# Sums of expert outputs by one product per 64 tokens, with loads that join both addends, and constant products around them

## What is computed

```python
y = jnp.zeros((t, dm), x2.dtype).at[flat_tok[order]].add(y_sorted)
...
xp = layer_norm(DEEPNORM_ALPHA * xp + hier_moe(xp, *moe_w), ln2_g[l], ln2_b[l])
```

## Time and profile before

| what | value |
|---|---|
| median of 3 runs | 2174.96 us (2174.8 to 2177.64) |
| the profiled execution | 2183.16 us, span 2181.3 us |
| PE busy | 2072.5 us, 95% of the span |
| DVE, ACT, POOL busy | 805.1, 325.7, 222.1 us |
| mean granted TensorE clock | 0.974 |
| all DMA | 535.92 MB, mean 246 GB/s |

### The profile page before, as it was taken

How to read it: one execution, slowest core, us unless ns; L and a number is a source line. 1 busy time by engine, 2 the same in 40 slices (tenths; PEclk the granted TensorE clock), 3 DMA queues, 4 the chain that set the end, 5 groups by cost and what they waited for, 6 DMA issues and landing times.

```text
span 2181.3 us, 32300 instructions
## 1 busy us (share of the span) xinstructions
PE 2072.5 (95%) x13024; PEld 1221.7 (56%) x13024; DVE 805.1 (37%) x1547; ACT 325.7 (15%) x856; POOL 222.1 (10%) x250
## 2 busy tenths in 40 slices
PE   8999999989999999899799999999999999999986
PEld 5666655565555655455366666555645556554542
DVE  4512166672222222222482123766622221222224
ACT  2011123311111011111010111333001110110103
POOL 1200000000111111110231000000001100111101
PEclk9999999999999999999899999999999999999997
DMA  6601131348999999998634101413689999999956
GB/s 223 193 30 38 41 128 68 113 158 316 360 392 400 414 384 396 392 387 334 231 123 120 39 29 32 158 59 116 228 325 391 399 406 395 392 388 394 379 219 236
DMA packets 77465, 535.92 MB, mean 246 GB/s; under 512 B 14586, under 2 KB 23674, under 8 KB 52386
## 3 DMA queue, kind: packets, MB, share of 16 engines
q1 hardware_dynamic: 64050, 498.37, 59.5%
q0 software_dynamic: 13264, 35.44, 4.8%
HBM read 494.14 MB, written 54.08 MB: 251 GB/s over the span
## 4 chain that ended last, share of the span: by engine, by line
PE 91%; DVE 4%; issue 3%; DMA 1%; ACT 1%; POOL 1%; DVEq 0%; SPq 0%; POOLq 0%
PE ps L925 20%; PE ps L616 19%; PE ps L969 10%; PE ps L763 9%; PE ps L905 6%; PE ps L595 4%; PE ps L893 3%; PE ps L976 3%; PE ps L921 3%; PE ps L949 2%; PE ps L567 1%; PE ps L963 1%; PE ps L569 1%; PE ps L805 1%; PE ps L705 1%
## 5 line engine op out<-in xcount | busy, mean ns | idle before, releaser
L927 PE MATMUL ps<-arena 128*64 128x256 f32 x1920 | 450.9, 391 | 0.0
L925 PE MATMUL ps<-arena 128*64 128x256 f32 x1920 | 450.9, 391 | 0.0
L616 PE MATMUL ps<-arena 128*128 128x344 f32 x1440 | 421.2, 453 | 0.0
L925 PEld LDWEIGHTS ps<-arena 128*64 128x64 f32 x1920 | 255.0, 135 | 175.9 <-issue 23.9
L616 PEld LDWEIGHTS ps<-arena 128*128 128x128 f32 x1440 | 272.0, 190 | 142.9 <-issue 3.6
L969 PE MATMUL ps<-arena 128*64 128x512 f32 x480 | 236.5, 639 | 22.3 <-issue 19.9
L927 PEld LDWEIGHTS ps<-arena 128*64 128x64 f32 x1920 | 254.5, 135 | 0.0
L971 PE MATMUL ps<-arena 128*64 128x512 f32 x480 | 236.8, 640 | 0.0
L763 PE MATMUL ps<-arena 128*128 128x512 f32 x448 | 195.9, 594 | 2.7 <-issue 2.7
L1703 DVE SCALAR_TENSOR_TENSOR arena<-ps,gates,arena 64x256 f32<-64x256 f32 (+1 forms) x128 | 60.9, 476 | 354.9 <-ACT arena L1228 354.9
L1970 POOL DMA_INDIRECT ytok<-arena,gidx x64 | 60.3, 942 | 955.3 <-DVE arena L1731 924.2
(11 more groups left out here) (262 smaller groups left out, 2133.0 us busy)
## 6 DMA issues: line engine op xcount, KB each, us to landing
arena<-in_w_gate SPq DMA_DIRECT2D x64, 2048.0 KB, 24.0
arena<-in_w_up SPq DMA_DIRECT2D x64, 2048.0 KB
arena<-in_w_down SPq DMA_DIRECT2D x64, 2048.0 KB
arena<-in_w_in SPq DMA_DIRECT2D x36, 512.0 KB, 3.5
ytok<-arena SPq DMA_DIRECT2D x32, 512.0 KB, 3.5
arena<-ytok SPq DMA_DIRECT2D x29, 512.0 KB, 9.3
arena<-out_y_all SPq DMA_DIRECT2D x16, 512.0 KB, 3.5
out_y_all<-arena SPq DMA_DIRECT2D x16, 512.0 KB
```

The lines of the kernel that those rows point to most:

```text
L616: last = mm(ps[:, 3 * half + ch, 0:CH], wring[:, slot, k * P:(k + 1) * P], xT[:, k, ch * CH:(ch + 1) * CH], start=(k == 0), stop=(k == KD ...
L925: mm(ps[HALF:P, 2 + q, 0:256], xgT[:, slot, k, 0:HALF], wg_half[slot3][q][:, k], start=(k == 0), stop=(k == KD - 1))
L927: last = mm(ps[0:HALF, 2 + q, 0:256], xgT[:, slot, k, 0:HALF], wu_half[slot3][q][:, k], start=(k == 0), stop=(k == KD - 1))
```

## The change

The rows are loaded and multiplied in another arrangement. For 64 tokens, one load brings both addends: the first ones to partitions 0 to 63, the second ones to partitions 64 to 127. A tile of 128 tokens still takes two loads of 512 KB (`xin[t]` for its first 64 tokens, `second[t]` for its last 64). A constant `both` of 128 by 64 (two identities above each other) then adds them in one product per 64 tokens and 512 columns; the two halves go to PSUM partitions 0 to 63 and 64 to 127. The sample tile takes one load of 16 rows. The loads of tiles 5 to 8 between the layers stay as they are. The ring behind layer 1 has three pairs in place of four. PE gets 24 constant products ahead of each series of sums and one behind each sum. Between the layers DVE scales tile 0 ahead of tile 1's statistics.

```diff
+        both = sb("both", [P, HALF])
+        both8 = sb("both8", [2 * NS, NS])
...
-                def second_in(t):
-                    sp.dma_start(second[t][0:tile_rows(t)], rows_of[T + t * P:T + t * P + tile_rows(t), :]
-                                 ).then_inc(s[f"l2_in{t}"], 16)
+                def both_in(t):
+                    if t == NB:
+                        sp.dma_start(both_s, a["ytok"][:, SEQ:T, :]
+                                     ).then_inc(s[f"l2_in{t}"], 16)
+                        return
+                    for tile, r0 in ((xin[t], t * P), (second[t], t * P + HALF)):
+                        sp.dma_start(tile, a["ytok"][:, r0:r0 + HALF, :]
+                                     ).then_inc(s[f"l2_in{t}"], 16)
...
+            def keep_busy(n, bank=5):
+                for _ in range(n):
+                    mm(ps[:, bank, 0:256], ident[:], masks[:, 0, :], start=True, stop=True)
...
-                ring = 4 if l == DEPTH - 1 else 2
+                ring = 3 if l == DEPTH - 1 else 2
...
                 for h in range(2):
-                    cols = slice(h * 512, (h + 1) * 512)
-                    mm(ps[0:rows, 2 * (t % ring) + h, :], ident[0:rows, 0:rows], xin[t][0:rows, cols],
-                       start=True, stop=False)
-                    last = mm(ps[0:rows, 2 * (t % ring) + h, :], ident[0:rows, 0:rows], second[t][0:rows, cols],
-                              start=False, stop=True)
+                    bank, cols = 2 * (t % ring) + h, slice(h * 512, (h + 1) * 512)
+                    if t == NB:
+                        last = mm(ps[0:NS, bank, :], both8[:], both_s[:, cols], start=True, stop=True)
+                    else:
+                        mm(ps[0:HALF, bank, :], both[:], xin[t][:, cols], start=True, stop=True)
+                        last = mm(ps[HALF:P, bank, :], both[:], second[t][:, cols], start=True, stop=True)
...
                     if l > 0:
                         outputs_summed(l - 1, t + 2)
+                        keep_busy(1, 7)
                     x_turned(t)
...
+                keep_busy(24, 3)
                 for t in range(2 if l < DEPTH - 1 else NT):
                     outputs_summed(l, t)
+                    keep_busy(1, 7)
...
                         shifted2(p - 1, rows_at[p - 1], p - 1)
+                        if p == 1:
+                            scaled2(0, rows_at[0], 0)
                         statistics2(p, rows_at[p], p)
-                        scaled2(p - 1, rows_at[p - 1], p - 1)
+                        if p > 1:
+                            scaled2(p - 1, rows_at[p - 1], p - 1)
```

More of the change, by code:

```diff
@@ L267, in build @@
         xin = [at(29552 + 1024 * t, DM) for t in range(NB)] + [at(27496, DM, parts=NS)]
-        second = [at(14448 + 1024 * t, DM) for t in range(4)] + [at(o, DM) for o in (37744, 38768, 39792, 28528)] \
-            + [at(26464, DM, parts=NS)]
+        second = [at(14448 + 1024 * t, DM) for t in range(4)] + [at(o, DM) for o in (37744, 38768, 39792, 28528)]
+        both_s = at(27496, DM, parts=2 * NS)
         FIRST3 = [(c, ch) for ch in range(NCH) for c in range(3)]
@@ L517, in first_in @@
                                  ).then_inc(s[f"l2_in{t}"], 16)
-                def second_in(t):
-                    sp.dma_start(second[t][0:tile_rows(t)], rows_of[T + t * P:T + t * P + tile_rows(t), :]
-                                 ).then_inc(s[f"l2_in{t}"], 16)
+                def both_in(t):
[6 more added lines that the diff above has]
+                                     ).then_inc(s[f"l2_in{t}"], 16)
                 if l < DEPTH - 1:
                     for t in range(SUMMED):
-                        first_in(t)
-                        second_in(t)
+                        both_in(t)
                         if 0 < t < SUMMED:
@@ L555, in _ @@
             settle(pe, s["pe_passed"])
+            def keep_busy(n, bank=5):
+                for _ in range(n):
+                    mm(ps[:, bank, 0:256], ident[:], masks[:, 0, :], start=True, stop=True)
             def outputs_summed(l, t):
-                rows = P if t < NB else NS
-                ring = 4 if l == DEPTH - 1 else 2
-                pe.wait_ge(s[f"l2_in{t}"], BASE + rows_in(l, t) + 32)
+                ring = 3 if l == DEPTH - 1 else 2
+                pe.wait_ge(s[f"l2_in{t}"], BASE + rows_in(l, t) + (32 if t < NB else 16))
                 if t >= ring:
@@ L848, in placed @@
                     last.then_inc(s["rk_inv"], 1)
-                def keep_busy(n):
-                    for _ in range(n):
-                        mm(ps[:, 5, 0:256], ident[:], masks[:, 0, :], start=True, stop=True)
                 early, late = slice(0, EARLY), slice(EARLY, NT)
@@ L1278, in summed @@
                 def summed(t, r):
-                    return ps[r, 2 * (t % 4):2 * (t % 4) + 2, :].rearrange("p a b -> p (a b)")
+                    return ps[r, 2 * (t % 3):2 * (t % 3) + 2, :].rearrange("p a b -> p (a b)")
                 def added2(t):
@@ L1331, in _ @@
                 step.mark(v.tensor_scalar(token[:, k, 0:1], tokens1[:, NB:NT], float(k * T - 1 - NONE), None, ALU.add))
+            step.mark(v.tensor_tensor(both[:], ident[:, 0:HALF], ident[:, HALF:P], ALU.add))
+            step.mark(v.tensor_tensor(both8[:], ident[0:2 * NS, 0:NS], ident[0:2 * NS, NS:2 * NS], ALU.add))
             step.mark(v.tensor_scalar(bias_row[:], rank_desc[:], NE - FIRST + 0.5, 1e6, ALU.is_gt, ALU.mult))
```

## The result

The changed kernel takes **2408.53 us** (median of 4 runs, 2403.78 to 2409.95), beside 2176.30 us of the kernel before (4 runs, 2174.8 to 2179.89): ratio on record 1.1051, 95% interval 1.1031 to 1.1071 (the two medians divided give 1.1067). The changed kernel's profiled execution has a span of 2407.2 us, 225.9 more than the 2181.3 before.

A forecast was written before the change was run, and what follows sets the result against it. PE was taken to bound the kernel, with 91% of the chain. 94.1 + 133.9 = 228.0 us took the profiled execution from 2183.16 to 2411.2; less 8.2 for the median gave 2403, range 2375 to 2450.

The forecast's parts named there:

- What bounds the kernel: PE holds 91% of the chain; the change acts only at the sums behind the last expert of each layer.
- Two engines per load: Changed `ytok` loads, outermost counts 2 and 128, get two DMA engines, the same two for all; weighed at 0.80.
- 10.22 us per load: Price of a changed load on two engines at 51.3 GB/s together, in place of 1.28 us.
- Between the layers: Tile 4 lands late, so layer 1's first projection starts at 1179.4 in place of 1085.27: +94.1 us.
- The 8.1 us for three accumulating loads: Between the layers, three POOL loads delay tile 4's landing by 2.7 us each; bounds 0 and 8.1.
- Behind layer 1: 16 slow loads land tile 7 at 2295.0; the span ends at 2315.2 in place of 2181.3: +133.9 us.
- The sample load's 1.3 us: Behind layer 1, the 64 KB sample load, one in place of two, adds 1.3 us after tile 7: 2296.3.
- The median: Whole kernel: profiled execution 2411.2 us, less 8.2 by which the earlier one lay above its median, gives 2403.
- The terms put at nothing: Between the layers, DVE's reordering, the earlier first tile and 24 constant products cost nothing, ending before tile 4 lands.
- The first: Rival, both places: loads keep 16 engines; tail 9.8 us earlier, boundary up to 5.5; 2162 us; chance 0.14.
- The second: Rival: 16 engines, but accumulating loads go ahead between the layers, 5 us loss there; 2170 us; chance 0.04.
- The third: Rival, at the summing products: the two column halves don't overlap; no size given; next to no chance.

The follow-up runs named there:

- e2_outer64: The changed kernel with the same loads walked token by token (outermost count 64) and the constant `both` fitted to that order; 2179.11 us, ratio 0.9999.
- e5_late_acc: e2_outer64 with POOL's accumulating loads issued later, tiles 5 and 6 behind tile 2, 7 behind 3, 8 behind 4; 2169.84 us, ratio 0.9954.
- e1_halves: The changed kernel with each load of both addends cut into two plain loads of 64 partitions each; 2195.49 us, ratio 1.0072.

## Why the prediction was right

**What bounds the kernel** held: 226 us went into the two places where PE waits or sums, and layer 1 between them moved by 2.2 us, as it does from run to run.

**Two engines per load** held. It was taken from one transfer with an outermost count of 127; the runs with counts 2, 4, 8 and 16 show it. The rule of the Trainium skill that the prediction cites (page "DMA: Bandwidth & Descriptors", section "Why a DMA increments its semaphore by 16 and not by 1") agrees with all four shares.

**10.22 us per load** came out as 10.04. Behind layer 1 the sums of two tiles in a row start 20.07 us apart, with two loads between (PE's timeline, columns as in the earlier trace rows, the first two of the eight):

```profile
2246.55 1.09 PE L578 MATMUL ps<-arena,both 128*64 128x512 f32 x1 [18.20 <-DMA arena<-ytok]
2266.63 1.09 PE L578 MATMUL ps<-arena,both 128*64 128x512 f32 x1 [15.25 <-DMA arena<-ytok]
```

The chosen price, from the rate of the row with 4 KB pieces, was the right one of the two: 22 GB/s per engine doesn't occur, it is 26.

**Between the layers**, +94.1 was forecast and +94.8 measured. Tile 4 was to land 116.5 us after the first load's issue (1172.5 less 1055.99) and landed after 117.0 (1174.69 less 1057.71). From landing to projection 7.05 us were measured, 6.9 forecast. The 8.1 us for three accumulating loads were the least certain term. The trace gives them as a remainder. In PE's timeline (columns as in the earlier trace rows) the sums of tiles 1, 2 and 3 start at

```profile
1101.46 1.09 PE L578 MATMUL ps<-arena,both 128*64 128x512 f32 x1 [16.63 <-DMA arena<-ytok]
1126.30 1.08 PE L578 MATMUL ps<-arena,both 128*64 128x512 f32 x1 [20.80 <-DMA arena<-ytok]
1150.86 1.08 PE L578 MATMUL ps<-arena,both 128*64 128x512 f32 x1 [18.48 <-DMA arena<-ytok]
```

and that of tile 4 at 1174.83: steps of 24.84, 24.56 and 23.97 us. Each holds two changed loads (20.07) and a plain one (1.28), and POOL issues one accumulating load in each (1103.20, 1127.97, 1152.52). What is left is 3.5, 3.2 and 2.6, together 9.3 us. So this term was 1.2 too low, ten loads at 0.18 less took 1.8 off again, and 1.1 came in the first two tiles; that the landing came within 0.5 us is partly luck.

**Behind layer 1**, +133.9 was forecast and +131.7 measured. From the first issue to tile 7's landing it is 163.5 us, where the working gives 165.8 (2295.0 less 2129.18): 16 loads at 0.18 less are 2.9. From the landing to the end it is 20.3 us, as in the working (2315.2 less 2295.0 is 20.2). The sample load's 1.3 us stand there in a sum of their own, 2296.3, but 2301.3 follows from 2295.0 without them, and rightly: in the chain the samples' product L576 follows the constant with no wait for a load.

**The median.** Forecast 2403, measured 2408.53, although the pieces came out 2.1 us smaller than forecast. The profiled execution was forecast at 2411.2 and took 2409.03. The forecast then took off the 8.2 us by which the profiled execution before lay above its median; the changed kernel's lay only 0.5 above. So that step, and not the mechanism, made the forecast 5.5 us low.

**The terms put at nothing** were nothing here only because the loads hid them. e2_outer64 uncovers them: the tail gains 8.1 us, and the boundary loses 2.7 us. The accumulating loads alone cost more than that, 6.9 us, as e5_late_acc shows.

**The rivals.** The first (16 engines, 2162) was right about the tail (-8.1, forecast -9.8) and wrong about the boundary: with full loads this change gives 2179, no change. The second, weighed at 0.04 beside 0.14, is what happens in that case, collision included: +5 and -9.8 were its pieces, +2.7 and -8.1 are measured; its 2170 was all the same 9 below the median. The third, halves that don't overlap, fell: in the trace after, L579 starts 0.01 to 0.04 us behind its L578. So if the loads had kept their engines, the forecast would have named the wrong one of the two.

## What to carry to other kernels

Read a DMA's outermost counts on both sides before anything else: `[2, 64, d]` into 128 partitions is two engines, and the same bytes as `[64, 2, d]` are sixteen; reorder what consumes the rows (here the columns of a constant matrix) to allow the second. A busy share of 1.0 isn't yet full rate, so look at the GB/s beside it, above all for loads to 64 partitions. When a faster stage lets transfers of another queue start sooner, check whether they now run ahead of the ones that TensorE waits for; holding them back gave here 0.45%, which neither the products nor the clock gave.

## What the runs showed of the hardware that was not expected

- Loads of 256 KB to 64 partitions move 229 GB/s with all 16 engines busy (e1_halves), the plain ones of 512 KB to 128 partitions 409 to 415.
- At 8 engines a load runs at 127 GB/s, hardly more than at 4 (104). With 16 as outermost count it is 236, with 64 (e2_outer64) and 128 it is above 400. Why is open.
- A clock of 1.00 in place of 0.50 in the first sums changed the end of the stretch between the layers by about 1 us (32.0 and 33.1), because tile 4's loads land equally late in both (25.6 and 25.7 us) and PE waits for them.
- Stretches that an edit doesn't touch differ by up to 8 us between profiled executions, more than twice the 0.13 to 0.15% (2.8 to 3.3 us) to either side that the intervals of 6 to 12 runs resolve.
